# Four tokens' one-hots by two VectorE comparisons, with the expert weights multiplied in by ScalarE

## The chip, the core and the metric

One core of a Trainium2 chip runs the whole program. The metric is the time of one execution in microseconds (us). TensorE (PE; its loads of weights are listed apart as PEld), VectorE (DVE), ScalarE (ACT) and GpSimd (POOL) each follow their own list of instructions strictly in order, and wait for each other through semaphores; SyncE (SP) issues the transfers from and to HBM.

## What is computed

The reference is two transformer blocks over 256 tokens of width 1024, one after the other: attention, a convolution, a state-space model, cross-attention and a feed-forward layer in the first; two recurrent mixers and a feed-forward layer with retrieved experts in the second. The change lies in that last layer:

```python
def peer_ffn(h, wq, keys, u_tab, v_tab):
    ...
        idx = i1 * PEER_NKEYS + i2
        g = jax.nn.softmax(best_s.astype(jnp.float32), axis=-1).astype(xb.dtype)
        act = jax.nn.gelu(jnp.einsum('tpkd,td->tpk', u_tab[idx], xb), approximate=False)
        return jnp.einsum('tpk,tpkd->td', g * act, v_tab[idx])
```

Each token has 8 heads with 16 picked experts, 128 picks in all; a pick is a pair of keys (i1, i2), each of 128, and a softmax weight g.

## The kernel before

The kernel does not gather experts. It runs all 16384 experts over all 256 tokens, in 128 tiles: tile c holds the 128 experts that share one of the two keys. For each token it needs a 128 x 128 table of weights by the two keys, which is zero but for the picked pairs. TensorE makes this table as a product of two one-hot matrices, with the 128 picks on the partitions: one side has a row of 128 with a 1 at the first key, multiplied by the weight g, and the other side a 1 at the second key. `idx[:, 0, t]`, `idx[:, 1, t]` and `idx[:, 2, t]` hold the two keys and the weight of token t, one pick on each partition; `iota` holds 0 to 127.

The stage that the change touches lies between the keys' retrieval and the second pass over the experts. Two jobs are interleaved in it by hand, on each engine in an order that is fixed when the program is written, as 32 rounds (g = 0 to 31):

- the tables of eight tokens, in two fours: `one_hot(n)` on VectorE, `expert_weights(n)` on TensorE (four products into a PSUM bank), `keep_weights` on ScalarE (copies the bank to `big`). n = 2g and 2g + 1;
- one or two of the tiles 76 to 119 of the first pass, by `u_before(g) = 76 + g * 44 // 32`: in 20 rounds one tile, in 12 rounds two. For tile c TensorE runs 24 products (`activations(c)`), ScalarE applies gelu and then rounds the tile c + 3 (`activate(c)`, which ends with `high_u(c + 3)`), and VectorE takes the rest that rounding left (`low_of`, called by `next_u`).

TensorE's round is: both fours, then the tiles. ScalarE's is: both copies, then gelu and rounding for each tile. VectorE's is: both fours of one-hots, then the rests. The one-hots have four places (`hot[n % 4]`, in two slots of the ring of tiles), so VectorE may be four fours ahead of TensorE; it waits on `expert_weights_made` for a place, and TensorE waits on `one_hot_ready` for the one-hots. The tiles of `peer_u` come by DMA from SyncE; the load of tile c + 4 is issued when `activations(c)` is done, into the place of tile c.

Of the kernel before, what the change touches and what calls it, by code (L numbers as in the profile page):

```python
# [6 lines left out]
ALU = mybir.AluOpType  # L7
ACT = mybir.ActivationFunctionType
# [6 lines left out]
P = 128  # L15
D = 1024
KD = D // P
T = 256
# [22 lines left out]
NE = 128  # L41
# [22 lines left out]
class Products:  # L64
# [8 lines left out]
    def add(self, key, takers, banked=True, upper=0):  # L73
        assert key not in self.number, key
        self.number[key] = self.count
        self.count += 1
        self.takers[key] = takers
        before = None
        if banked:
            b = BANKS * upper + self.turn[upper] % BANKS  # L80
            self.turn[upper] += 1
            before, self.in_bank[b] = self.in_bank[b], key
            self.bank[key] = b
        for r in takers:
            self.takes[r] = self.takes.get(r, 0) + 1
            self.rank[key, r] = self.takes[r]
        return before
# [28 lines left out]
def program(nc, d):  # L116
# [6 lines left out]
    with ExitStack() as ctx:  # L123
# [4 lines left out]
        def sem(name):  # L128
            return ctx.enter_context(nc.semaphore(name))
# [27 lines left out]
        places, at = {}, 0  # L157
        for place in sorted(FIRST_HIGH + (XO_LOW, XO_HIGH, MIXED)):
            places[f"gap{at}"], places[place] = [P, place - at], [P, SLOT]
            at = place + SLOT  # L160
# [4 lines left out]
        ident, iota = tables[:, 0], tables[:, 1]  # L165
        idx = whole["idx"]
# [3 lines left out]
        def col(name, i=0, parts=P):  # L170
            at, n = COLS[name]
            assert i < n
            return par[0:parts, at + i:at + i + 1]
# [134 lines left out]
        hot = [half_slots[:, n, :].rearrange("p (n s e) -> p n s e", n=4, s=2) for n in (10, 11, 4, 5)]  # L308
# [37 lines left out]
        def flag(name):  # L346
            if name not in flags:
                flags[name] = sem(name)
            return flags[name]
# [13 lines left out]
        def u_before(g):  # L363

            return G_AT + g * (U_AT - G_AT) // (T // 8)

        def emptied(slot):

            return released[max(n for n in range(len(items)) if n % RING == slot)]
# [1053 lines left out]
        def _(dve):  # L1423
            v = nc.vector
# [68 lines left out]
            for g in range(2):  # L1493
                rows, at = slice(64 * g, 64 * g + 64), slice(16 * g, 16 * g + 16)
# [6 lines left out]
                last = v.tensor_scalar(cc[rows, 2, :, at], c_im[rows], -1.0, None, ALU.mult)  # L1501
# [48 lines left out]
            for a in range(2):  # L1550
                last = v.scalar_tensor_tensor(conv[:, a, :], bank[:, 0:T], -1.0 / 256, conv[:, a, :], ALU.mult, ALU.add)
# [4 lines left out]
            for c in range(NS):  # L1556
                for i in range(2):
                    last = v.tensor_tensor_scan(rot[:, i, c, :], s_mag[:, c:c + 1].to_broadcast([P, T]), rot[:, i, c, :],
                                                0.0, ALU.mult, ALU.add)
# [12 lines left out]
            for a in range(2):  # L1572
                last = v.scalar_tensor_tensor(ys[:, a, :], u[:, a, :], col("ssm_d", a), bank[:, a * T:(a + 1) * T],
                                              ALU.mult, ALU.add)
# [9 lines left out]
            for i in (0, 2, 1, 3):  # L1584
                bank = s.product(("qk_r", i))
                g = col("sbq_g") if i < 2 else col("sbk_g")
# [68 lines left out]
            for key, at, src, n in (("ssm_sum", 0, ys, 2), ("conv_sum", 1, cvo, 2), ("sb_sum", 0, None, 4)):  # L1655
                r = reciprocal_std(key, T, at)
                first_ = {"ssm_sum": 6, "conv_sum": 4, "sb_sum": 0}[key]
                for i in range(n):
                    dst = mixed[:, first_ + i, :]
                    last = v.scalar_tensor_tensor(dst, dst if src is None else src[:, i, :], col("branch_g", first_ + i), r,  # L1660
                                                  ALU.mult, ALU.mult)
# [151 lines left out]
            for i in range(4):  # L1813
# [3 lines left out]
                last = v.tensor_tensor(two, two, sums[:, 2 * i:2 * i + 2, :], ALU.add)  # L1817
# [28 lines left out]
            one = lambda r: ones[r, 0:1].to_broadcast([r.stop - r.start, T])  # L1846
# [29 lines left out]
            def short_conv(dst, src, c):  # L1876
                w0, w1, w2 = (col("conv_w", 8 * j + c) for j in range(3))
                link(v.tensor_scalar(dst, src, w1, None, ALU.mult))
                spans = []
                if dst.shape[1] == 2 * T:  # L1880
                    spans.append((dst[:, 1:T], src[:, 0:T - 1], dst[:, 0:T - 1], src[:, 1:T]))
                    dst, src = dst[:, T:2 * T], src[:, T:2 * T]
                d4, s4 = (t.rearrange("p (r n) -> p r n", n=64) for t in (dst, src))
                spans.append((d4[:, :, 1:], s4[:, :, :-1], d4[:, :, :-1], s4[:, :, 1:]))
                for d1, s1, _, _ in spans:
                    last = v.scalar_tensor_tensor(d1, s1, w0, d1, ALU.mult, ALU.add)
                link(last)
                for _, _, d1, s1 in spans:
                    last = v.scalar_tensor_tensor(d1, s1, w2, d1, ALU.mult, ALU.add)
                return last  # L1890

            half_low(5, 6, 7)
            for c in range(MH):
                s.after(("mk", c), "act")
                last = short_conv(mk_t[:, c, :], mk_raw[:, c, :], 4 + c)
# [6 lines left out]
            def convolved_query(c):  # L1902
                s.after(("mq", c // 2), "act")
                return short_conv(mq_t[:, c, :], mq_raw[:, c, :], c)
# [11 lines left out]
            for c in range(1, 4):  # L1916
                last = convolved_query(c)
# [6 lines left out]
            for i in range(4):  # L1924
# [3 lines left out]
                last = v.tensor_tensor_scan(a, r, b, 0.0, ALU.mult, ALU.add)  # L1928
            link(last)
            for dr in range(2):  # L1930
# [4 lines left out]
                for i in (2 * dr, 2 * dr + 1):  # L1935
                    lat = cs[:, i, T:].rearrange("p (c n) -> p c n", n=GC)
                    mid = lat[:, :, 32 - dr:33 - dr]
                    last = v.tensor_tensor(q_in[:, i, :].rearrange("p (c n) -> p c n", n=GC), lat,
                                           mid.to_broadcast([P, 4, GC]), ALU.subtract)
# [87 lines left out]
            for j in range(2):  # L2027
                half = slice(64 * j, 64 * j + 64)
                last = v.tensor_copy(q_z[half, j], q_st[half])
            last.then_inc(flag("q_split"), 1)  # L2030
            half_low(24, 25)
            for i in range(4):
# [7 lines left out]
                for n, c in enumerate(order):  # L2040
                    dst = st[:, i, order[0], :] if n == 3 else run_s
                    if n == 0:
                        last = v.tensor_copy(dst, add(c))
                    else:
                        last = v.scalar_tensor_tensor(dst, run_s, e_end[:, i, c:c + 1], add(c), ALU.mult, ALU.add)
                    link(last)
                for n, c in enumerate(order[:3]):
                    last = v.scalar_tensor_tensor(st[:, i, order[n + 1], :], st[:, i, c, :], e_end[:, i, 4 + c:5 + c],
                                                  add(4 + c), ALU.mult, ALU.add)
# [7 lines left out]
            for i in range(4):  # L2057
                r = reciprocal_std(("mix2_sum", i), 512, i % 2)
                for j in range(2):
                    c = 2 * i + j  # L2060
                    g_ = col("ml_g", c) if c < 4 else col("gla_g", c - 4)
                    last = v.scalar_tensor_tensor(mix2[:, c, :], mix2[:, c, :], g_, r[:, j * T:(j + 1) * T], ALU.mult, ALU.mult)
# [18 lines left out]
            for i in range(4):  # L2081
                bank = s.product(("mix2_out", i))
                for j in range(2):
                    k = 2 * i + j
                    last = v.scalar_tensor_tensor(x[:, k, :], bank[:, j * T:(j + 1) * T], mod[:, 2, k, 0:1], x[:, k, :],
                                                  ALU.mult, ALU.add)
# [120 lines left out]

            dve.wait_ge(made, emptied(RING - 1))
            dve.wait_ge(made, emptied(2))
            hot_ready, w_made = flag("one_hot_ready"), flag("expert_weights_made")  # L2210

            def one_hot(n):

                if n >= 4:
                    dve.wait_ge(w_made, n - 3)
                for q in range(4):
                    at = 4 * n + q
                    v.tensor_scalar(hot[n % 4][:, q, 0, :], iota, idx[:, 0, at:at + 1], idx[:, 2, at:at + 1],  # L2218
                                    ALU.is_equal, ALU.mult)
                last = v.tensor_tensor(hot[n % 4][:, :, 1, :], iota.unsqueeze(1).broadcast_to([P, 4, NE]),  # L2220
                                       idx[:, 1, 4 * n:4 * n + 4].unsqueeze(2).broadcast_to([P, 4, NE]), ALU.is_equal)
                last.then_inc(hot_ready, 1)

            s.after(("keys3", 0), "act")
            for g in range(T // 8):
# [68 lines left out]
        def _(act):  # L2294
            a_ = nc.scalar.activation
# [10 lines left out]
            def copy_out(key, dst, src=None, scale=1.0):  # L2306
                bank = s.product(key)
                s.took(key, a_(dst, bank if src is None else src(bank), ACT.Copy, scale=scale))  # L2308
# [25 lines left out]
            for c in range(NS):  # L2334
                last = a_(trig[:, 1, c, :], ramp, ACT.Copy, scale=sm[:, 5, c:c + 1])
# [285 lines left out]
            for dr in range(2):  # L2621
                last = a_(e_end[:, 2 * dr:2 * dr + 2, :], ends[:, dr, :, :, 63 if dr == 0 else 0], ACT.Exp)
# [43 lines left out]
            for j in range(2):  # L2666
                bank = s.product(("att", j))
                for odd in range(2):
                    r = slice(64 * odd, 64 * odd + 64)
                    n = bank[r].rearrange("p (m t) -> p m t", t=GC)  # L2670
                    dst = att[r, j].rearrange("p d b h t -> p (d b h) t")[:, :, odd * GC:(odd + 1) * GC]
                    last = a_(dst, n, ACT.Copy)
# [52 lines left out]
            w_made, w_read = flag("expert_weights_made"), flag("expert_weights_read")  # L2725
# [46 lines left out]
            def keep_keys(b):  # L2772

                copy_out(("keys3", b), idx[:, :, b * P:(b + 1) * P], lambda bk: bk[:, 0:3 * P].rearrange("p (i t) -> p i t", i=3))

            def keep_weights(t, n, half):

                act.wait_ge(w_made, n + 1)
                a_(g_all[:, t:t + 4, :], ps[:, 2 + half, :].rearrange("p (t e) -> p t e", e=NE), ACT.Copy).then_inc(w_read, 1)
# [14 lines left out]
            for b in range(TB):  # L2794
                for g in range(4):
                    copy_out(("psc", b, g), psc[:, b, 4 * g:4 * g + 4, :].rearrange("p j e -> p (j e)"),
                             scale=token_inverse[:, b:b + 1])
# [12 lines left out]
            activated(EXP_AT[1] // 4, G_AT // 4)  # L2810
            for g in range(T // 8):
                for half in range(2):
                    keep_weights(8 * g + 4 * half, 2 * g + half, half)
                if g == 2:
                    keep_keys(1)
                for c in range(u_before(g), u_before(g + 1)):
                    activate(c, c % 4, c // 4)
# [261 lines left out]
```

## Time and profile before

| what | value |
|---|---|
| runs | 1558.75 us median of 3 (1558.55 to 1563.71) |
| the profiled execution's own time | 1558.66 us |
| its span, from the first to the last instruction | 1556.9 us |
| TensorE matmul busy | 1531.8 us, 98% |
| VectorE busy | 1180.3 us, 76% |
| ScalarE busy | 767.1 us, 49% |
| TensorE's mean granted clock | 0.997 |

The profiled execution's own time is 1.76 us above its span, and 0.09 us below the median. All shares are means over the whole program, whose stages have different limits; a busy TensorE is not TensorE at its peak, since the ends of matmuls are modelled.

### The profile page before, as it was taken

How to read it: one execution, taken by the hardware profiler on the slowest of the kernel's cores; microseconds unless marked ns; L12 is line 12 of the kernel's file. 1: busy time of each engine (PE TensorE's matmuls, PEld its weight loads, DVE VectorE, ACT ScalarE, POOL GpSimd, SP SyncE). 2: the span in 40 equal slices, each digit the busy share in tenths (PEclk: the TensorE clock that was granted, in tenths of full speed). 3: DMA queues.
4: the chain of work that ended last, by engine and by line, in shares of the span. 5: the costliest groups of instructions: out<-in, count | busy, mean ns of one | idle time of the engine just before them, and what ended most of it. 6: DMA issues, size and time to landing. Idle time of an engine off the chain costs nothing.

```text
span 1556.9 us, 28174 instructions
## 1 busy us (share of the span) xinstructions
PE 1531.8 (98%) x10460; PEld 1385.4 (89%) x10460; DVE 1180.3 (76%) x2029; ACT 767.1 (49%) x1089; POOL 60.4 (4%) x108
## 2 busy tenths in 40 slices
PE   8999999999999999999999999999999999999997
PEld 6678897999999887989999999999999888888886
DVE  7997645776646968757699999988875777777776
ACT  5237544544435563425444654544545545545543
POOL 2002000100000034000000000000000000000000
PEclk9999999999999999999999999999999999999999
DMA  7364658455533230516277777555558777777763
GB/s 298 118 242 158 241 228 318 160 190 185 175 128 104 94 109 1 204 55 243 73 231 221 231 225 218 171 168 153 157 156 294 254 243 242 238 241 243 238 202 95
DMA packets 95942, 293.66 MB, mean 189 GB/s; under 512 B 10480, under 2 KB 45424, under 8 KB 82928
## 3 DMA queue, kind: packets, MB, share of 16 engines
q1 hardware_dynamic: 95712, 292.21, 56.3%
q8 instruction: 60, 0.98, 0.3%
q14 instruction: 26, 0.21, 0.0%
q10 hardware_dynamic: 144, 0.26, 0.0%
HBM read 274.60 MB, written 17.83 MB: 188 GB/s over the span
## 4 chain that ended last, share of the span: by engine, by line
PE 92%; DVE 4%; DMA 2%; ACT 1%; issue 0%; SPq 0%; POOL 0%; DVEq 0%; POOLq 0%
PE ps L479 92%; DVE split_ring L2136 1%; DMA ring<-kept_acts 1%; DMA ring<-in_peer_u 1%; DMA ring<-in_w_in 1%; DVE big L1996 0%; DVE big L2184 0%; DVE big L2188 0%; DVE big L2186 0%; DMA ring<-in_w_gv 0%; DMA kept_acts<-par 0%; ACT split_ring L2735 0%; ACT split_hid_high L2719 0%; PE ps L863 0%; DVE x L2284 0%
## 5 line engine op out<-in xcount | busy, mean ns | idle before, releaser
L479 PE MATMUL ps<-split_hh,split_ring 128*128 128x256 f32 (+1 forms) x3632 | 516.0, 291 | 3.1 <-DVE split_ring L2136 2.9
L479 PEld LDWEIGHTS ps<-split_hh,split_ring 128*128 128x128 f32 x3632 | 456.9, 191 | 14.2 <-DVE split_ring L2136 1.9
L479 PE MATMUL ps<-split_ring 128*128 128x512 f32 (+1 forms) x1472 | 370.2, 382 | 3.0 <-DVE split_ring L2136 3.0
L479 PEld LDWEIGHTS ps<-split_ring 128*128 128x128 f32 x1472 | 268.7, 188 | 58.1 <-DVE split_ring L2136 4.9
L2136 DVE TENSOR_TENSOR split_ring<-ring,split_ring 128x1024 fp32r<-128x1024 f32 x196 | 238.6, 1220 | 49.4 <-ACT split_ring L2735 48.0
L2735 ACT ACTIVATE split_ring<-ring 128x1024 fp32r<-128x1024 f32 x128 | 135.1, 1057 | 78.9 <-DMA ring<-in_peer_u 78.5
L2239 DVE TENSOR_TENSOR ring<-ring,big 128x256 f32<-128x256 f32 x128 | 81.4, 637 | 81.5 <-PE ps L479 70.3
L479 PE MATMUL ps<-split_ffn_h,split_ffn_w 128*128 128x256 f32 x1056 | 127.4, 283 | 0.0
L479 PEld LDWEIGHTS ps<-split_ffn_h,split_ffn_w 128*128 128x128 f32 x1056 | 127.0, 192 | 0.1
L2742 ACT ACTIVATE split_ring<-ring 128x1024 fp32r<-128x1024 f32 x68 | 72.2, 1062 | 94.8 <-PE ps L479 81.5
L1741 DVE TENSOR_TENSOR split_ffn_w<-ring,split_ffn_w 128x2048 fp32r<-128x2048 f32 x33 | 75.6, 2291 | 49.8 <-ACT split_ffn_w L2535 49.8
L479 PE MATMUL ps<-split_hid_high,split_ffn_w 128*128 128x258 f32 (+1 forms) x736 | 112.0, 284 | 0.2
L479 PEld LDWEIGHTS ps<-split_hid_high,split_ffn_w 128*128 128x128 f32 x736 | 102.0, 191 | 1.1 <-ACT split_hid_high L2719 1.0
L2742 ACT ACTIVATE split_ring<-hh 128x1024 fp32r<-128x1024 f32 x60 | 63.8, 1064 | 75.1 <-PE ps L479 74.9
L479 PE MATMUL ps<-big 128*128 128x256 f32 (+11 forms) x632 | 82.5, 327 | 3.3 <-ACT big L2308 1.3
L479 PEld LDWEIGHTS ps<-big 128*128 128x128 f32 (+5 forms) x632 | 64.7, 165 | 23.0 <-issue 10.6
L2308 ACT ACTIVATE big<-ps 128x512 f32<-128x512 f32 (+2 forms) x62 | 28.7, 481 | 110.7 <-PE ps L479 91.1
L2535 ACT ACTIVATE split_ffn_w<-ring 128x2048 fp32r<-128x2048 f32 x33 | 63.1, 1912 | 40.1 <-PE ps L479 40.1
L2218 DVE TENSOR_SCALAR ring<-tables,idx 128x128 f32<-128x128 f32 x256 | 71.3, 344 | 5.9 <-PE ps L479 5.9
L2136 DVE TENSOR_TENSOR split_hh<-hh,split_ring 128x1024 fp32r<-128x1024 f32 x60 | 73.1, 1218 | 0.0
L479 PE MATMUL ps<-ring 128*128 128x128 f32 x512 | 62.4, 275 | 0.0
L479 PEld LDWEIGHTS ps<-ring 128*128 128x128 f32 x512 | 60.0, 192 | 0.0
(350 smaller groups left out, 2007.6 us busy)
## 6 DMA issues: line engine op xcount, KB each, us to landing
ring<-in_peer_u SPq DMA_DIRECT2D x128, 512.0 KB, 3.9
ring<-in_peer_v SPq DMA_DIRECT2D x68, 512.0 KB, 3.5
hh<-in_peer_v SPq DMA_DIRECT2D x60, 512.0 KB, 3.5
ring<-in_w_mod SPq DMA_DIRECT2D x24, 1024.0 KB, 5.7
ring<-in_ffn_in SPq DMA_DIRECT2D x22, 1024.0 KB, 4.9
ring<-kept_acts SPq DMA_DIRECT2D x128, 128.0 KB, 3.1
ring<-in_ffn_out SPq DMA_DIRECT2D x11, 1024.0 KB, 4.8
ring<-in_w_out SPq DMA_DIRECT2D x8, 1024.0 KB, 9.2
```

The source lines that it names most:

```text
L479: return nc.tensor.matmul(out, lhsT, rhs, start=start, stop=stop, skip_group_check=True)
L1741: v.tensor_tensor(fw_low[:, q, :], ring[:, (ffn_at + n) % RING, :], fw_high[:, q, :].bitcast(F32), ALU.subtract).then_inc(flag("weights_sp ...
L2136: v.tensor_tensor(low, tile, high.bitcast(F32), ALU.subtract).then_inc(flag(kind + "_split"), 1)
L2218: v.tensor_scalar(hot[n % 4][:, q, 0, :], iota, idx[:, 0, at:at + 1], idx[:, 2, at:at + 1], ALU.is_equal, ALU.mult)
L2239: v.tensor_tensor(weighted_[:, q, :], act_in[:, q, :], g_, ALU.mult).then_inc(flag("whole_weighted"), 1)
L2308: s.took(key, a_(dst, bank if src is None else src(bank), ACT.Copy, scale=scale))
L2535: a_(fw_high[:, n % 3, :], ring[:, at % RING, :], ACT.Copy).then_inc(flag("weights_rounded"), 1)
L2735: a_(u_high[q], u_tile[:, q, :], ACT.Copy).then_inc(flag("u_high_ready"), 1)
L2742: a_(v_high[q % 4], v_tile[q], ACT.Copy).then_inc(flag("v_high_ready"), 1)
```

## The change

`one_hot(n)` no longer has four `tensor_scalar` instructions (one to a token, each comparing and multiplying by the weight) and a `tensor_tensor` for the other side. It has two `tensor_tensor` comparisons, one for each side, each over four tokens, and raises a new semaphore, `one_hot_marked`. A new function on ScalarE, `weigh_one_hots(n)`, waits for it, multiplies the first side of the four tokens by their weights in place, a token at a time, and raises `one_hot_ready`, for which TensorE waits as before. It is called for n = 0 and 1 ahead of the first copy, and then for n = 2g + half + 1 ahead of the copy of each four.

```diff
             def one_hot(n):
 
                 if n >= 4:
                     dve.wait_ge(w_made, n - 3)
-                for q in range(4):
-                    at = 4 * n + q
-                    v.tensor_scalar(hot[n % 4][:, q, 0, :], iota, idx[:, 0, at:at + 1], idx[:, 2, at:at + 1],
-                                    ALU.is_equal, ALU.mult)
-                last = v.tensor_tensor(hot[n % 4][:, :, 1, :], iota.unsqueeze(1).broadcast_to([P, 4, NE]),
-                                       idx[:, 1, 4 * n:4 * n + 4].unsqueeze(2).broadcast_to([P, 4, NE]), ALU.is_equal)
-                last.then_inc(hot_ready, 1)
+                for side_ in range(2):
+                    last = v.tensor_tensor(hot[n % 4][:, :, side_, :], iota.unsqueeze(1).broadcast_to([P, 4, NE]),
+                                           idx[:, side_, 4 * n:4 * n + 4].unsqueeze(2).broadcast_to([P, 4, NE]), ALU.is_equal)
+                last.then_inc(flag("one_hot_marked"), 1)
...
+            def weigh_one_hots(n):
+
+                act.wait_ge(flag("one_hot_marked"), n + 1)
+                for q in range(4):
+                    one = hot[n % 4][:, q, 0, :]
+                    last = a_(one, one, ACT.Copy, scale=idx[:, 2, 4 * n + q:4 * n + q + 1])
+                last.then_inc(flag("one_hot_ready"), 1)
...
             for g in range(T // 8):
                 for half in range(2):
+                    if (g, half) == (0, 0):
+                        weigh_one_hots(0)
+                    if 2 * g + half + 1 < T // 4:
+                        weigh_one_hots(2 * g + half + 1)
                     keep_weights(8 * g + 4 * half, 2 * g + half, half)
```

How the lists stand then, at the start of the stage. First ScalarE before: L2779 is the copy of a four (`keep_weights`), L2756 gelu, L2735 the rounding of a tile (`high_u`); rounds 0 and 1 and the start of round 2.

```order
L2779 ACTIVATE big<-ps 128x512 [waits expert_weights_made] x2
L2756 ACTIVATE par<-ps 128x256 [waits act_out0,activations_made]
L2735 ACTIVATE split_ring<-ring 128x1024 [waits activations_made,u_in3]
L2779 ACTIVATE big<-ps 128x512 [waits expert_weights_made] x2
L2756 ACTIVATE acts<-ps 128x256 [waits act_out1,activations_made]
L2735 ACTIVATE split_ring<-ring 128x1024 [waits activations_made,u_in0]
L2779 ACTIVATE big<-ps 128x512 [waits expert_weights_made] x2
```

The same place on ScalarE now; its line numbers are those of the changed kernel: L2778 is the multiplication, L2784 the copy, L2753 gelu, L2732 the rounding. Round 0 and the start of round 1.

```order
L2778 ACTIVATE ring<-ring,idx 128x128 [waits one_hot_marked]
L2778 ACTIVATE ring<-ring,idx 128x128 x3
L2778 ACTIVATE ring<-ring,idx 128x128 [waits one_hot_marked]
L2778 ACTIVATE ring<-ring,idx 128x128 x3
L2784 ACTIVATE big<-ps 128x512 [waits expert_weights_made]
L2778 ACTIVATE ring<-ring,idx 128x128 [waits one_hot_marked]
L2778 ACTIVATE ring<-ring,idx 128x128 x3
L2784 ACTIVATE big<-ps 128x512 [waits expert_weights_made]
L2753 ACTIVATE par<-ps 128x256 [waits act_out0,activations_made]
L2732 ACTIVATE split_ring<-ring 128x1024 [waits activations_made,u_in3]
L2778 ACTIVATE ring<-ring,idx 128x128 [waits one_hot_marked]
L2778 ACTIVATE ring<-ring,idx 128x128 x3
```

The multiplications of fours 0, 1 and 2 are in round 0; the last two rows, those of four 3, open round 1 and stand behind the gelu and the rounding of round 0's tile.

TensorE's list is the same before and now; these are rounds 0 and 1, where the products of 128x128 are the fours and those of 128x256 the tiles.

```order
L479 MATMUL ps<-ring 128x128 [waits one_hot_ready]
L479 MATMUL ps<-ring 128x128 x3
L479 MATMUL ps<-ring 128x128 [waits one_hot_ready]
L479 MATMUL ps<-ring 128x128 x3
L479 MATMUL ps<-split_hh,split_ring 128x256 [waits activations_read,u_split]
L479 MATMUL ps<-split_hh,split_ring 128x256 x23
L479 MATMUL ps<-ring 128x128 [waits expert_weights_read,one_hot_ready]
L479 MATMUL ps<-ring 128x128 x3
L479 MATMUL ps<-ring 128x128 [waits expert_weights_read,one_hot_ready]
L479 MATMUL ps<-ring 128x128 x3
```

Nothing moved here; only the engine that raises `one_hot_ready` is another.

## Rows read from the trace of the kernel before

**Rows 1.** The page's first part: busy us, share of the span, instructions.
```profile
PE 1531.8 (98%) x10460; PEld 1385.4 (89%) x10460; DVE 1180.3 (76%) x2029; ACT 767.1 (49%) x1089; POOL 60.4 (4%) x108
```
**Rows 2.** The stage as one window: us, busy us of each engine, clock, DMA.
```profile
980.00:1165.00 185.00, 185.00 (x1581) 185.00 (x1581) 158.73 (x369) 93.47 (x154) 0.00 (x0) 1.00 0.54 160
```
**Rows 3.** Waits of TensorE in the whole program: us, times, longest us.
```profile
PE ps L479 <- ACT big L2299: 6.5, 2, 5.9
PE ps L479 <- DVE split_ring L2136: 5.9, 9, 1.9
```
**Rows 4.** Groups of instructions in the stage: busy us, mean ns, idle before, releaser.
```profile
L2218 DVE TENSOR_SCALAR ring<-tables,idx 128x128 f32<-128x128 f32 x248 | 69.1, 344 | 5.9 <-PE ps L479 5.9
L479 PEld LDWEIGHTS ps<-ring 128*128 128x128 f32 x498 | 58.5, 192 | 0.0
L2220 DVE TENSOR_TENSOR ring<-tables,idx 128x512 f32<-128x512 f32 x63 | 43.3, 687 | 0.0
```
**Rows 5.** Timeline, a round after one tile: start us, us, engine, line.
```profile
1034.68 1.88 PEld L479 LDWEIGHTS ps<-ring 128*128 128x128 f32 x16
1035.00 0.38 ACT L2756 ACTIVATE acts<-ps 128x256 f32<-128x256 f32 x1 [1.57 <-PE ps L479]
1035.28 1.05 ACT L2735 ACTIVATE split_ring<-ring 128x1024 fp32r<-128x1024 f32 x1
1036.22 1.16 ACT L2779 ACTIVATE big<-ps 128x512 f32<-128x512 f32 x2
...
1039.34 0.42 PEld L479 LDWEIGHTS ps<-ring 128*128 128x128 f32 x3
```
**Rows 6.** Timeline, a round after two tiles.
```profile
1109.66 1.88 PEld L479 LDWEIGHTS ps<-ring 128*128 128x128 f32 x16
...
1111.18 1.06 ACT L2735 ACTIVATE split_ring<-ring 128x1024 fp32r<-128x1024 f32 x1 [0.82 <-DMA ring<-in_peer_u]
...
1112.14 0.58 ACT L2779 ACTIVATE big<-ps 128x512 f32<-128x512 f32 x1
```
**Rows 7.** Timeline, the first round.
```profile
983.78 1.88 PEld L479 LDWEIGHTS ps<-ring 128*128 128x128 f32 x16
...
986.01 1.06 ACT L2735 ACTIVATE split_ring<-ring 128x1024 fp32r<-128x1024 f32 x1 [1.53 <-DMA ring<-in_peer_u]
...
986.97 0.58 ACT L2779 ACTIVATE big<-ps 128x512 f32<-128x512 f32 x1
```
**Rows 8.** Timeline, the last round's start.
```profile
1160.24 1.88 PEld L479 LDWEIGHTS ps<-ring 128*128 128x128 f32 x16
```
**Rows 9.** ScalarE: copies multiplied by a number per partition, on the timeline, back to back.
```profile
14.51 3.29 ACT L2335 ACTIVATE big<-big 128x256 f32<-128x256 f32 x8
```
**Rows 10.** ScalarE by shapes, whole program: busy us, mean ns, idle before.
```profile
L2335 ACT ACTIVATE big<-big 128x256 f32<-128x256 f32 x8 | 3.3, 492 | 0.0
L2642 ACT ACTIVATE big<-big 128x256 f32<-128x256 f32 x8 | 3.3, 412 | 0.6 <-DVE big L1970 0.6
L2642 ACT ACTIVATE big<-big 128x128 f32<-128x128 f32 x8 | 2.5, 308 | 1.2 <-DVE big L1970 1.1
```
**Rows 11.** Timeline, a load of weights that waited for ScalarE.
```profile
36.19 0.60 ACT L2308 ACTIVATE big<-ps 128x512 f32<-128x512 f32 x1 [5.24 <-PE ps L622]
36.84 0.31 PEld L479 LDWEIGHTS ps<-big 32*128 32x128 f32 x6 [0.93 <-ACT big L2308]
```
**Rows 12.** Windows in which TensorE stood or had few partitions; columns as in rows 2.
```profile
35.00:40.00 5.00, 3.70 (x32) 2.87 (x32) 4.93 (x7) 2.59 (x6) 0.00 (x0) 0.97 0.59 210
40.00:45.00 5.00, 5.00 (x14) 2.65 (x12) 4.96 (x14) 4.48 (x7) 0.00 (x0) 0.50 0.00 0
45.00:50.00 5.00, 5.00 (x12) 2.05 (x11) 5.00 (x14) 1.42 (x1) 0.00 (x0) 0.84 0.00 0
1535.00:1540.00 5.00, 3.59 (x15) 2.82 (x16) 2.83 (x4) 1.36 (x4) 0.00 (x0) 1.00 0.00 0
```

More of the change, by code:

```diff
@@ L2209, in _ @@
             dve.wait_ge(made, emptied(2))
-            hot_ready, w_made = flag("one_hot_ready"), flag("expert_weights_made")
+            w_made = flag("expert_weights_made")
             def one_hot(n):
```

## The prediction

> **What bounds the kernel now.** I read the page's busy times first: TensorE is busy for 98% of the span, VectorE 76%, ScalarE 49% [rows 1]. Then the stage that the change touches, as one window: in its 185 us TensorE is busy for all 185, VectorE 158.7, ScalarE 93.5, at a granted clock of 1.00, the upper level of 2.4 GHz [rows 2]. The list of waits says the same from the other side: in the whole program TensorE waited 5.9 us, in nine pieces, for VectorE's rests of tiles, and its longest wait is the 5.9 us before its first product [rows 3]; none of its waits lies in this stage. So TensorE sets the pace, and an edit counts here only if it takes work from TensorE or makes it wait. The change takes nothing from TensorE. What is left to ask is when the one-hots become ready, and for that I went to the timeline of single rounds.
>
> A round begins when TensorE loads the first weights of its two fours. After a round of one tile that is 1034.68, and the next round begins at 1039.34, 4.66 us later [rows 5]. The sixteen loads of the two fours take 1.88 us from the first start to the last end, and one takes 0.192 us [rows 4, 5], so they start (1.88 - 0.192) / 15 = 0.113 us apart, and the second four begins 8 x 0.113 = 0.90 us after the first. ScalarE in the same round: gelu starts at 1035.00, because it needs the tile that TensorE has just finished; rounding starts at 1035.28; the copies start at 1036.22 [rows 5]. ScalarE is thus free for something new 1.54 us after the round began, and that is 0.64 us after TensorE wants its second four.
>
> **The change part by part.** VectorE loses four comparisons a four and gains one. The old ones cost 69.1 / 248 = 0.28 us each as they overlap, 1.11 us a four, against 0.69 us for one comparison over four tokens [rows 4]. That is 0.43 us a four, about 27 us over 64 fours. I cost it at nothing: TensorE does not wait for VectorE in this stage, and VectorE's only waits at the one-hots, 5.9 us, are for TensorE to free a place [rows 4], so it already runs as far ahead as its four places allow. A faster VectorE waits longer for a place.
>
> ScalarE gains 256 multiplications of 128 numbers by a number per partition. No row shows that shape. The nearest row is the same operation, from and to SBUF, on 256 numbers: eight in a row took 3.29 us at 0.492 us each, so they start (3.29 - 0.492) / 7 = 0.400 us apart [rows 9, 10]. For 128 numbers instead of 256 I take off what another ScalarE line saves by that, 0.412 - 0.308 = 0.104 us [rows 10]: 0.388 us each, 0.296 us apart. A four's multiplications then end 3 x 0.296 + 0.388 = 1.28 us after the first starts, and hold ScalarE for 4 x 0.296 = 1.18 us. From above, the row of 256 as it stands gives 3 x 0.400 + 0.492 = 1.69 us. From below, the row of 128 without a number per partition, with the same overlap of 0.092, gives 3 x 0.216 + 0.308 = 0.96 us. I take 1.28, since the nearer row is the same operation. From the last end to TensorE's load goes another 0.05 us: a copy that ended at 36.79 released a load at 36.84 [rows 11].
>
> Now where these stand. Four 2g + 2 is multiplied in round g, between the two copies, long before TensorE asks for it: after 1.54 us, the other four's 1.18, a copy of about 0.55 and its own 1.28 it is ready some 4.6 us after the round began, and TensorE's next round then begins no sooner than 6.6 us after. It costs nothing; without that cover of about 2 us it would cost its own 1.28 us. The other four, 2g + 1, opens ScalarE's round g. It stands behind gelu and rounding of the last tile of round g - 1, and TensorE wants it right behind its first four. Queued behind it on ScalarE are the copies, whose banks TensorE needs only a round later; queued behind TensorE's wait are all tiles of the round, so the wait is TensorE's own and shifts everything that follows.
>
> - After a round of one tile: multiplications start when the copies started, 1036.22; end and release at 1036.22 + 1.28 + 0.05 = 1037.55. TensorE wants them at 1034.68 + 0.90 = 1035.58. Wait: 1.97 us [rows 5].
> - After a round of two tiles the rounding itself waits 0.82 us for a tile's load, since its two tiles follow each other without a pause; the copies start at 1112.14, and 1112.14 + 1.33 - (1109.66 + 0.90) gives 2.91 us [rows 6].
> - The first round has both fours in front: the copies started at 986.97, so fours 0 and 1 are through at 986.97 + 1.18 + 1.28 + 0.05 = 989.48, against 983.78 + 0.90 = 984.68. Wait: 4.80 us [rows 7].
>
> By the rule of `u_before`, 20 rounds have one tile and 12 have two; the last round's two tiles precede no four, so there are 20 waits of the first kind, 11 of the second and one of the third. The trace confirms the count: from 983.78 to 1160.24 are 176.46 us [rows 7, 8], of which 31 x 4.66 = 144.5 leaves 32.0, or 2.9 us for each of 11 second tiles. Sum: 20 x 1.97 + 11 x 2.91 + 4.80 = 39.4 + 32.0 + 4.8 = **76.2 us**. The profiled execution's own time is 1558.66 us, 0.09 below the median, so the forecast is 1558.66 + 76.2 = 1634.9, **1635 us**.
>
> The Trainium skill speaks against such an edit: in "ScalarE: Activation LUTs", section "Rules for kernel authors", it sends plain multiplications to VectorE. The rows agree in direction (0.28 us as part of a comparison on VectorE, 0.30 us as an extra instruction on ScalarE), but by that rule alone the 76 us of multiplications on a ScalarE that is busy for half of the stage would be hidden, and the time 1559; the wait comes from their place in the list, of which the rule says nothing.
>
> Can the delay be absorbed later? TensorE's waits for rests of tiles are 5.9 us in the whole program [rows 3]; even if all came after this stage and vanished, that is the most that could be given back.
>
> **The rivals.** *VectorE was the pace after all* (not slower). If TensorE's full 185 us only hid a pace set by VectorE, the 27 us taken from VectorE would come off: about 1558.7 - 27 = 1532 us, or, with TensorE's wait covered, 1559. It decides only if four 2g + 1 is multiplied before TensorE wants it, which means a start by 1035.58 - 1.33 = 1034.25, before the gelu at 1035.00 that stands ahead of it in the list [rows 5]. For it speaks VectorE's 86% in the stage, against it the order on ScalarE. Chance 0.04.
>
> *The clock falls.* TensorE's granted clock fell once inside the program: after 35 to 40 us, where it was busy for 3.70 of 5 us and in part with products of 32 partitions, it was at 0.50 (1.2 GHz) and then 0.84, so about 6.6 us at the lower level, worth some 3.3 us [rows 12]. Now TensorE would work 4.66 of 6.63 us, 70%, in a round of one tile. Against the rival: from 1535 to 1540 us it was busy for 3.59 of 5 us, 72%, and kept 1.00 [rows 12]. The first wait, 4.8 us, is longer than any shown with the clock kept up and may cost those 3.3 us once, 1638. Should the clock fall after each of the 11 longer waits, 11 x 3.3 = 36 us come on top, 1671; after all 32, 106 us, 1741. Chance of more than a few drops 0.08. The Trainium skill has the rule for it in "TensorE: Matmul & The Clock Gate", section "Why this matters for your kernels": long idle gaps between bursts of matmuls bring the lower clock back. By that rule the first gap is the one in danger.
>
> *Part of the wait goes away.* If the loads of tiles land sooner, because the slower stage asks less of the DMA, the 11 longer waits shrink towards 1.97: 11 x 0.94 = 10 us less, 1625. For it speaks that the DMA's mean share is 0.54 in the stage [rows 2]; against it, the two tiles of such a round still follow each other at the old distance, and each load is issued as before. Chance 0.08, and it lies inside the range.
>
> **How the numbers follow.** The forecast's mechanism, with the wait of about 2 to 3 us a round, has 0.88 with the third rival, the clock 0.08, the not slower rival 0.04. Its bounds: the multiplications at 0.96 or 1.69 us change 33 fours (32 waits, the first with two) by -0.32 or +0.41 us, -10.6 or +13.5 us, so 1624 to 1649. The loads' 10 us and part of the 5.9 us below, one drop of the clock above, make the range **1614 to 1655**; it leaves out most of the clock's rival and all of the other, 0.12, and some tails. A measurement of this kernel cannot tell less than about 0.5%, 7.8 us, from no change. Every case but the first rival's two ends is slower by more than that: slower 0.96, same 0.02, faster 0.02.
>
> **What would show it.** On TensorE's list of waits, ScalarE's multiplications should be new and first, with 32 pieces and 70 to 80 us in all, the longest near 4.8; the stage should last about 76 us longer with TensorE's busy time unchanged. A round after one tile should take 6.6 us instead of 4.66. On ScalarE a multiplication should take 0.39 us, four of them 1.28, and the one that releases TensorE should follow a rounding, never a wait for VectorE; VectorE should wait longer for places. After the stage, windows of the second pass should be the same, later. I am wrong if TensorE's waits sum to far from 76 us, if the multiplications wait for VectorE's marks, or if the granted clock in the stage is visibly below 1.00.

## The result and the profile after

The changed kernel takes 1638.37 us (median of 4 runs, 1636.70 to 1640.81) against 1559.02 us before (median of 4): 1.0505 times as long, 95% interval 1.0492 to 1.0518. The forecast was 1635 us, between 1614 and 1655. Its profiled execution took 1640.81 us, the longest of the four, with a span of 1639.1 us and a mean granted clock of 0.993.

The page's first part, which answers to [rows 1]:

```profile
PE 1546.6 (94%) x10460; PEld 1395.4 (85%) x10460; DVE 1156.3 (71%) x1837; ACT 838.6 (51%) x1345; POOL 60.5 (4%) x108
```

ScalarE has 71.5 us and 256 instructions more, VectorE 24 us less. TensorE has the same 10460 products, is busy for 14.8 us more and stands idle for longer. TensorE's waits in the whole program, which answer to [rows 3] (us, times, longest):

```profile
PE ps L479 <- ACT ring L2778: 65.2, 32, 4.2
PE ps L479 <- DVE split_ring L2136: 7.0, 10, 1.9
```

A new releaser heads the list, ScalarE's multiplication (L2778 of the changed kernel), with 32 pieces, one to a round. VectorE's rests of tiles cost what they did, within about 1 us. By shapes, in the stage, ScalarE has no idle time ahead of a multiplication, so none waited for VectorE's marks; VectorE waits 29.7 us for places where it waited 5.9 [rows 4]:

```profile
L2778 ACT ACTIVATE ring<-ring,idx 128x128 f32<-128x128 f32 x254 | 80.4, 389 | 0.0
L2217 DVE TENSOR_TENSOR ring<-tables,idx 128x512 f32<-128x512 f32 x124 | 78.9, 686 | 29.7 <-PE ps L479 29.7
```

Now a round after one tile, from the timeline (L2753 is gelu, L2732 the rounding); it answers to [rows 5]:

```profile
1045.87 0.98 PEld L479 LDWEIGHTS ps<-ring 128*128 128x128 f32 x8
...
1046.19 0.38 ACT L2753 ACTIVATE par<-ps 128x256 f32<-128x256 f32 x1 [2.75 <-PE ps L479]
...
1046.47 1.05 ACT L2732 ACTIVATE split_ring<-ring 128x1024 fp32r<-128x1024 f32 x1
...
1047.42 1.26 ACT L2778 ACTIVATE ring<-ring,idx 128x128 f32<-128x128 f32 x4
...
1048.73 0.97 PEld L479 LDWEIGHTS ps<-ring 128*128 128x128 f32 x8 [1.88 <-ACT ring L2778]
```

The sixteen loads that stood together have fallen into two groups of eight. The multiplications start 1.55 us after the round began (before, the copies started after 1.54), last 1.26 us, and 0.05 us after they end TensorE loads the second four. It does so 2.86 us into the round instead of 0.90: 1.96 us late, where 1.97 was forecast.

The first round, which answers to [rows 7], and a round after two tiles, which answers to [rows 6]:

```profile
987.80 2.43 ACT L2778 ACTIVATE ring<-ring,idx 128x128 f32<-128x128 f32 x8
989.12 3.48 PEld L479 LDWEIGHTS ps<-ring 128*128 128x128 f32 x16 [4.44 <-ACT ring L2778]
...
1036.74 0.98 PEld L479 LDWEIGHTS ps<-ring 128*128 128x128 f32 x8
...
1038.46 1.06 ACT L2732 ACTIVATE split_ring<-ring 128x1024 fp32r<-128x1024 f32 x1 [1.02 <-DMA ring<-in_peer_u]
1039.42 1.26 ACT L2778 ACTIVATE ring<-ring,idx 128x128 f32<-128x128 f32 x4
...
1040.73 1.78 PEld L479 LDWEIGHTS ps<-ring 128*128 128x128 f32 x8 [3.01 <-ACT ring L2778]
1042.39 3.55 PEld L479 LDWEIGHTS ps<-split_hh,split_ring 128*128 128x128 f32 x24
```

In both, the loads after the wait are slow: sixteen take 3.48 us where the round before the change took 1.88, eight take 1.78 us instead of 0.97. The windows of the stage say why (columns as in [rows 2]; the first number after the five engines is the granted clock):

```profile
990.00:1000.00 10.00, 8.31 (x61) 8.12 (x61) 6.66 (x9) 6.77 (x19) 0.00 (x0) 0.87 0.23 68
1000.00:1010.00 10.00, 8.31 (x70) 8.12 (x69) 4.41 (x7) 6.09 (x16) 0.00 (x0) 1.00 0.22 66
1010.00:1020.00 10.00, 7.59 (x52) 7.40 (x51) 4.95 (x6) 5.32 (x13) 0.00 (x0) 0.83 0.45 133
1030.00:1040.00 10.00, 7.80 (x64) 7.61 (x64) 4.28 (x7) 5.45 (x13) 0.00 (x0) 1.00 0.49 147
1040.00:1050.00 10.00, 7.58 (x51) 7.39 (x52) 5.72 (x9) 6.74 (x20) 0.00 (x0) 0.83 0.31 90
...
1100.00:1110.00 10.00, 7.65 (x53) 7.46 (x53) 4.95 (x6) 5.73 (x13) 0.00 (x0) 0.83 0.46 131
...
1210.00:1220.00 10.00, 6.91 (x45) 6.72 (x46) 4.43 (x7) 6.74 (x19) 0.00 (x0) 0.83 0.31 104
```

After some of the waits the clock was at the lower level, 1.2 GHz, for a while: around the first round, and in four windows of ten us that show 0.83 in the mean. Over the whole stage it was 0.97:

```profile
980.00:1250.00 270.00, 204.83 (x1616) 198.72 (x1615) 136.53 (x178) 169.07 (x413) 0.00 (x0) 0.97 0.38 113
```

The second pass over the experts is as it was, only later: 300 us from 1280 hold 299.07 us of TensorE at 1.00, as 300.00 of the 300 us from 1200 did before.

```profile
1280.00:1580.00 300.00, 299.07 (x1320) 247.28 (x1318) 234.31 (x336) 153.28 (x225) 0.00 (x0) 1.00 0.77 248
```

### The profile page after: what moved, and what is told of

The parts are those of the page before. It is cut to its first block, busy times and chain, and to the rows that moved or that the text cites. A ratio compares the mean times of both kernels' runs of the same rounds, so it can differ in the third digit from the quotient of the medians.

```text
span 1639.1 us, 28238 instructions
## 1 busy us (share of the span) xinstructions
PE 1546.6 (94%) x10460; PEld 1395.4 (85%) x10460; DVE 1156.3 (71%) x1837; ACT 838.6 (51%) x1345; POOL 60.5 (4%) x108
## 4 chain that ended last, share of the span: by engine, by line
PE 79%; DVE 9%; ACT 5%; DMA 5%; issue 1%; SPq 0%; POOL 0%; DVEq 0%; POOLq 0%; ACTq 0%
PE ps L479 78%; DMA ring<-in_peer_u 3%; ACT ring L2778 2%; ACT split_ring L2732 2%; DVE big L1533 1%; DVE split_ring L2136 1%; DMA ring<-kept_acts 1%; DVE big L1558 1%; DMA ring<-in_peer_v 0%; DVE big L1996 0%; DVE big L1440 0%; DVE big L2184 0%; DVE big L2188 0%; DVE big L2186 0%; DMA ring<-in_w_gv 0%
## 5 line engine op out<-in xcount | busy, mean ns | idle before, releaser
L2732 ACT ACTIVATE split_ring<-ring 128x1024 fp32r<-128x1024 f32 x128 | 135.1, 1056 | 98.9 <-DMA ring<-in_peer_u 98.4
L2236 DVE TENSOR_TENSOR ring<-ring,big 128x256 f32<-128x256 f32 x128 | 81.2, 635 | 81.1 <-PE ps L479 70.5
L479 PE MATMUL ps<-ring 128*128 128x128 f32 x512 | 75.1, 293 | 65.2 <-ACT ring L2778 65.2
L479 PEld LDWEIGHTS ps<-ring 128*128 128x128 f32 x512 | 66.4, 202 | 71.3 <-ACT ring L2778 71.3
L2217 DVE TENSOR_TENSOR ring<-tables,idx 128x512 f32<-128x512 f32 x128 | 81.4, 686 | 29.7 <-PE ps L479 29.7
L2739 ACT ACTIVATE split_ring<-hh 128x1024 fp32r<-128x1024 f32 x60 | 63.9, 1064 | 75.1 <-PE ps L479 75.1
L2778 ACT ACTIVATE ring<-ring,idx 128x128 f32<-128x128 f32 x256 | 80.9, 389 | 0.0
```

The lines of the kernel that those rows point to most:

```text
L479: return nc.tensor.matmul(out, lhsT, rhs, start=start, stop=stop, skip_group_check=True)
L2217: last = v.tensor_tensor(hot[n % 4][:, :, side_, :], iota.unsqueeze(1).broadcast_to([P, 4, NE]), idx[:, side_, 4 * n:4 * n + 4].unsqueeze( ...
L2236: v.tensor_tensor(weighted_[:, q, :], act_in[:, q, :], g_, ALU.mult).then_inc(flag("whole_weighted"), 1)
L2732: a_(u_high[q], u_tile[:, q, :], ACT.Copy).then_inc(flag("u_high_ready"), 1)
L2739: a_(v_high[q % 4], v_tile[q], ACT.Copy).then_inc(flag("v_high_ready"), 1)
L2778: last = a_(one, one, ACT.Copy, scale=idx[:, 2, 4 * n + q:4 * n + q + 1])
```

## The experiments

Two theories: **place** (TensorE waits because four 2g + 1 is multiplied behind the gelu and the rounding of the tile that TensorE has just finished) and **load** (ScalarE got too much to do, or a chain over two engines costs wherever it stands). A third, that VectorE had been the pace, was the prediction's rival on the other side.

**The multiplications a round ahead.** The same work on the same engines; only ScalarE's order differs.

```diff
                     if (g, half) == (0, 0):
                         weigh_one_hots(0)
-                    if 2 * g + half + 1 < T // 4:
-                        weigh_one_hots(2 * g + half + 1)
+                        weigh_one_hots(1)
                     keep_weights(8 * g + 4 * half, 2 * g + half, half)
+                    if 2 * g + half + 2 < T // 4:
+                        weigh_one_hots(2 * g + half + 2)
```

> The same work on every engine as in the changed kernel; ScalarE multiplies both fours of round g + 1 in round g, each behind a copy, so that none stands behind the gelu and the rounding of the round's last tile. Theory 'place': the 31 waits of 2 to 3 us go, only the first round's wait of 4 to 6 us stays, with at most one drop of the clock; about 1567 us (1562 to 1575), if ScalarE's round of some 4.6 us just fits into TensorE's 4.66 us. Theory 'load' (ScalarE has too much to do, or a chain over two engines costs wherever it stands): above 1600 us.

Measured: 1569.25 us, 1.0056 times the kernel before (1.0034 to 1.0078). TensorE's waits for the multiplications fell from 65.2 us in 32 pieces to 4.0 in 2, as the list of waits says:

```profile
PE ps L479 <- ACT ring L2778: 4.0, 2, 3.8
```

By its windows the stage's middle has TensorE busy for 99.45 of 100 us, beside a ScalarE that is busy for 86.32:

```profile
980.00:1000.00 20.00, 16.20 (x126) 15.99 (x124) 15.13 (x23) 14.15 (x36) 0.00 (x0) 0.91 0.43 129
1000.00:1100.00 100.00, 99.45 (x839) 98.44 (x838) 69.96 (x92) 86.32 (x218) 0.00 (x0) 1.00 0.52 155
```

So 69 of the 79 us are the price of the order alone, and not of ScalarE's work. A wait of 3.8 us in the first round and the lower clock behind it are left.

**An even four twice, an odd four twice.** The changed kernel with four more multiplications, into a PSUM bank that nobody reads, for one four of each round. The edit is that for the even fours; for the odd ones the condition is `n % 2 == 1`.

```diff
                 act.wait_ge(flag("one_hot_marked"), n + 1)
+                if n % 2 == 0:
+                    act.wait_ge(chain["act"], s.n)
+                    for q in range(4):
+                        last = a_(ps[:, 6, q * NE:(q + 1) * NE], hot[n % 4][:, q, 0, :], ACT.Copy, scale=idx[:, 2, 4 * n + q:4 * n + q + 1])
+                    s.n += 1
+                    last.then_inc(chain["act"], 1)
```

> The changed kernel, with the four multiplications of each even four (2g, between the copies) made a second time, into a PSUM bank that nobody uses: about 1.2 us more on ScalarE in each round. Theory 'place': it lies in the cover of some 2 us before TensorE asks for that four, so 1638 us, as without it (1633 to 1645). Theory 'load': 32 x 1.2 = 38 us more, about 1676 us.

> The same as the even one, but for the odd fours (2g + 1, behind the rounding). Theory 'place': each of the 32 waits grows by 1.2 us, 38 us in all, so about 1676 us, and more where the granted clock falls after the longer waits (1670 to 1720). Theory 'load': as the even one, by the same amount. A large difference between the two speaks for the place.

Measured: 1643.70 us (1637.54 to 1644.67) with the even fours twice, 1706.66 us (1704.71 to 1707.24) with the odd ones; without either 1638.37. The same work costs some 5 us in one place and 68 in the other. With the even fours, TensorE's wait for the multiplications is what it was, and the extra work (L2779) went into ScalarE's own idle time ahead of the next gelu, which shrank from 1.98 us to 0.82 for the same tile. That gelu in the changed kernel; then, with the even fours twice, TensorE's wait (L2784 is the multiplication here) and a stretch of ScalarE's timeline (L2790 is the copy):

```profile
1052.80 0.38 ACT L2753 ACTIVATE acts<-ps 128x256 f32<-128x256 f32 x1 [1.98 <-PE ps L479]
```

```profile
PE ps L479 <- ACT ring L2784: 66.1, 32, 4.8
```

```profile
1044.12 1.24 ACT L2779 ACTIVATE ps<-ring,idx 128x128 f32<-128x128 f32 x4
...
1045.29 1.28 ACT L2784 ACTIVATE ring<-ring,idx 128x128 f32<-128x128 f32 x4
1046.46 0.59 ACT L2790 ACTIVATE big<-ps 128x512 f32<-128x512 f32 x1
1047.87 0.38 ACT L2753 ACTIVATE acts<-ps 128x256 f32<-128x256 f32 x1 [0.82 <-PE ps L479]
```

With the odd fours the waits grew by 101.6 - 65.2 = 36.4 us, as expected. The two profiled executions differ by 1704.71 - 1640.81 = 63.9 us, so 27.5 are left, and they come with the granted clock: its mean over the 320 us of the stage is 0.86, where it was 0.97 over the 270 us of the changed kernel's stage. On TensorE's timeline, 20 of its stretches from a wait to the next round are 1.5 to 2.5 us longer than the same stretch at full clock, some 35 us in all; in the changed kernel there are five, with 7.3 us in all. The wait and the window:

```profile
PE ps L479 <- ACT ring L2784: 101.6, 33, 4.0
```

```profile
980.00:1300.00 320.00, 221.27 (x1517) 215.06 (x1516) 133.15 (x172) 199.83 (x525) 0.00 (x0) 0.86 0.31 90
```

**VectorE's part alone.** The two comparisons stay, ScalarE's multiplications go, and TensorE waits for the comparisons directly.

```diff
-                last.then_inc(flag("one_hot_marked"), 1)
+                last.then_inc(flag("one_hot_ready"), 1)
...
-                    if (g, half) == (0, 0):
-                        weigh_one_hots(0)
-                    if 2 * g + half + 1 < T // 4:
-                        weigh_one_hots(2 * g + half + 1)
```

> Only VectorE's part of the change: two comparisons a four, and no multiplication by the weights at all (left out), so TensorE waits for VectorE's marks directly. Theory 'place' with VectorE off the path: 1559 us, as before the change (1556 to 1563), although VectorE has some 27 us less to do. Rival 'VectorE was the pace': about 1532 us.

Measured: 1559.00 us, 0.9997 times the kernel before (0.9987 to 1.0006). From 985 to 1160 us VectorE was busy for 127.2 us, where it had been for 152.6 before the change. Taking work from VectorE is worth nothing here; the rival that saw VectorE as the pace falls.

**GpSimd multiplies.** ScalarE's list is that of before; GpSimd takes a whole four in one instruction. (The edit is against the changed kernel.)

```diff
-                    if (g, half) == (0, 0):
-                        weigh_one_hots(0)
-                    if 2 * g + half + 1 < T // 4:
-                        weigh_one_hots(2 * g + half + 1)
...
+            for n in range(T // 4):
+                pool.wait_ge(flag("one_hot_marked"), n + 1)
+                four_ = hot[n % 4][:, :, 0, :]
+                g.tensor_tensor(four_, four_, idx[:, 2, 4 * n:4 * n + 4].unsqueeze(2).broadcast_to([P, 4, NE]), ALU.mult)\
+                    .then_inc(flag("one_hot_ready"), 1)
```

> VectorE's two comparisons as in the changed kernel, but GpSimd, which has nothing else to do in the stage, multiplies a whole four by its weights in one instruction; ScalarE's list is that of before. Theory 'place': nothing stands ahead of the multiplication on its engine, and two of some 1.3 us (its 128x512 addition took 1.296 us before) fit into a round of 4.66 us, so TensorE waits in the first round at most: 1559 to 1563 us. Theory 'a chain over two engines costs wherever it stands': 1600 us and more.

Measured: 1561.87 us, 1.0024 times the kernel before (1.0013 to 1.0036). Here a chain over two engines costs some 3 us, not 79: its second engine has nothing else ahead of the multiplication, and TensorE waits 1.6 us, in 2 pieces, for it.

**The first two fours earlier.** The round-ahead order, with the first round's multiplications placed earlier too. (The edit is against the round-ahead kernel.)

```diff
-            activated(EXP_AT[1] // 4, G_AT // 4)
+            for c in range(EXP_AT[1], G_AT - 1):
+                activate(c, c % 4, c // 4)
+            weigh_one_hots(0)
+            activate(G_AT - 1, 3, G_AT // 4 - 1, more=False)
+            weigh_one_hots(1)
+            high_u(G_AT + 2, 2, G_AT // 4)
             for g in range(T // 8):
                 for half in range(2):
-                    if (g, half) == (0, 0):
-                        weigh_one_hots(0)
-                        weigh_one_hots(1)
```

> The round-ahead order, and in addition the first two fours are multiplied one tile earlier: the first before the gelu of tile 75, the second between this gelu and the rounding of tile 78. Theory 'place': the first wait falls from 3.8 us to about 1.5 and the drop of the clock behind it goes, so some 4 us less than the round-ahead order, about 1564 us (1560 to 1567). If what the round-ahead order has left over comes from ScalarE being nearly full, it stays at 1568 us or more.

Measured: 1562.82 us, 1.0029 times the kernel before (1.0014 to 1.0045). The wait of the first round fell from 3.8 us to 0.9, and the stage's first 20 us kept the clock at 1.00, by the list of waits and the window:

```profile
PE ps L479 <- ACT ring L2778: 1.2, 2, 0.9
```

```profile
980.00:1000.00 20.00, 18.81 (x159) 18.42 (x158) 18.27 (x28) 17.68 (x47) 0.00 (x0) 1.00 0.54 162
```

None of the six kernels is faster than the kernel before: TensorE was full in this stage, and no version takes work from it.

## Why the prediction was right

- **The mechanism** was the forecast's: odd fours behind gelu and rounding, on TensorE's own path. The order alone (the round-ahead kernel) and the price by place (even against odd) show it; the odd fours' extra 1.2 us came back as 36.4 us of waits over 32 rounds. ScalarE's multiplications never waited for VectorE, as forecast.
- **The price of a multiplication** was right. Forecast from the row of 256 numbers: 0.388 us each, 1.28 us for four. Measured: 0.389 us each (254 in the stage) and 1.26.
- **The waits** were a little too large: 1.97 us after one tile (measured 1.96), 2.91 after two, 4.80 in the first round (measured 4.44). The list of waits gives 65.2 us where 70 to 80 were forecast, because it counts idle time alone. Before, a round's sixteen products were busy for 1.95 us in one piece; now they are for 1.06 + 1.16 us in two. So a wait delays TensorE by some 0.27 us more than the list says: 1.69 + 0.27 = 1.96 after one tile. The rounds after two tiles are the mis-sized term. Their listed waits are 2.35 to 2.82 us, 2.47 in the mean of eleven, which makes 2.74. The sixteen products before, and one of the shortest waits now, on TensorE's timeline:

```profile
1034.80 1.95 PE L479 MATMUL ps<-ring 128*128 128x128 f32 x16
```

```profile
1055.48 1.06 PE L479 MATMUL ps<-ring 128*128 128x128 f32 x8
1058.88 1.16 PE L479 MATMUL ps<-ring 128*128 128x128 f32 x8 [2.35 <-ACT ring L2778]
```

  In these eleven rounds the rounding waited 0.67 us in the mean for its tile's load. The forecast had taken one round of before, with 0.82; the mean of the eleven rounds before was 0.78. So a little of the third rival, loads that land sooner, came true; why they did is open. The waits make 20 x 1.96 + 11 x 2.74 + 4.44 = 73.8 us, against 76.2.
- **The clock** was the term that the sum put at nothing; the range allowed for one drop after the first wait. A clock visibly below 1.00 in the stage was one of the forecast's own signs of being wrong, and it came: 0.97 in the mean, with five drops. It fell behind the first wait and behind four of the eleven waits that follow two tiles, never behind one of the twenty shorter ones. From the load at 1040.73 to the next round's at 1045.87 are 5.14 us for a four and a tile; the same work at full clock took 3.75, on TensorE's timeline:

```profile
1023.50 0.97 PEld L479 LDWEIGHTS ps<-ring 128*128 128x128 f32 x8 [1.88 <-ACT ring L2778]
...
1027.25 0.98 PEld L479 LDWEIGHTS ps<-ring 128*128 128x128 f32 x8
```

  At about 1.4 to 1.6 us each, five drops make some 7.3 us. So the rival in which the clock falls came true in part, at less than half of the 3.3 us a drop that it had been priced at. TensorE's busy time, forecast as unchanged, rose by 14.8 us, about what these drops and 0.27 us at each of the 32 waits make.
- **The sum.** Together 73.8 + 7.3 = 81.1 us of the 82.15 that the two profiled executions differ by. The two errors had opposite signs, so that the forecast came out only 3 us below the median is in part luck; below the profiled execution it was 6 us.
- **The cover of the even fours** held: about 1.2 us more work there left TensorE's waits unchanged. That kernel's median stands 5 us above the changed one's, but its profiled execution took 1637.54 us at a mean granted clock of 0.995, and the three others, at 0.990 to 0.992, took 1643.66 to 1644.67. The changed kernel's four had 0.993 to 0.995. So the 5 us go with a lower clock; whether the extra work brought that about is not shown.
- **Nothing from VectorE**: shown by the kernel without multiplications.
- The rule of the Trainium skill that sends plain multiplications to VectorE (in "ScalarE: Activation LUTs", "Rules for kernel authors") pointed the right way, but the price did not come from the engine: the same 256 multiplications on ScalarE cost 79 us in one order and 4 in another.

## What to carry to other kernels

An engine's list is a queue: work that is handed to an engine with idle time costs nothing while it is done before its consumer wants it; past that moment, what stands ahead of it at that place counts as well as its own time (1.54 us and 1.33 us here, less the 0.90 until TensorE wants it). Before moving a step, find on the timeline when its consumer wants it, and what its new engine waits for just before; a step that stands behind something the consumer itself has just released turns the idle time into a wait of the consumer. Where it must go there, put it one round ahead.

## What the runs showed of the hardware

**The clock fell in gaps that looked harmless.** In the changed kernel's stage TensorE's twenty waits of 1.69 us never brought the lower clock; those of 2.35 to 2.82 us did in four of eleven cases. Their length alone does not tell which: one of 2.35 us did, and one of 2.73 did not. With the odd fours doubled the stage's mean fell to 0.86. The Trainium skill says in "TensorE: Matmul & The Clock Gate", section "Why this matters for your kernels", that long idle gaps between bursts bring the lower clock back. By that rule the first wait of 4.2 us alone seemed in danger; the measured windows at 0.83 go further than that.

**GpSimd slowed VectorE.** Comparisons and rests on VectorE, in the kernel without multiplications and, below it, in that with GpSimd (by shapes, 985 to 1160 us; busy us, mean ns):

```profile
L2217 DVE TENSOR_TENSOR ring<-tables,idx 128x512 f32<-128x512 f32 x124 | 77.3, 686 | 8.3 <-PE ps L479 8.3
L2136 DVE TENSOR_TENSOR split_ring<-ring,split_ring 128x1024 fp32r<-128x1024 f32 x44 | 53.8, 1224 | 39.5 <-ACT split_ring L2732 39.3
```

```profile
L2217 DVE TENSOR_TENSOR ring<-tables,idx 128x512 f32<-128x512 f32 x124 | 120.1, 1026 | 0.0
L2136 DVE TENSOR_TENSOR split_ring<-ring,split_ring 128x1024 fp32r<-128x1024 f32 x43 | 61.0, 1437 | 0.4 <-ACT split_ring L2732 0.4
```

The same comparison took 1.026 us instead of 0.686 in the mean, and VectorE was busy for 174.6 of these 175 us, where it had been for 152.6 before the change, as the windows show (before, then with GpSimd):

```profile
985.00:1160.00 175.00, 175.00 (x1497) 175.00 (x1496) 152.58 (x354) 88.94 (x146) 0.00 (x0) 1.00 0.54 159
```

```profile
985.00:1160.00 175.00, 174.70 (x1487) 174.34 (x1488) 174.64 (x167) 88.59 (x146) 104.69 (x62) 1.00 0.53 157
```

GpSimd itself took 1.69 us a four, where 1.3 was expected. The Trainium skill states in "GPSIMD Engine Reference", section "Key points", that GpSimd shares its ways into SBUF with VectorE and contends with VectorE's instructions that have two inputs there; the rows agree. TensorE waited only 1.6 us for GpSimd in all, but moving that work off VectorE gave VectorE more busy time than it had before the change.
